# Evictions a step later, two sigmoid buffers, and conv coefficients on GpSimd in a hybrid encoder block

## The reference, cut to what matters

```
z = rms_norm(h)                     # h: 16 meta tokens + 4096 positions, 1024 channels, batch 4
v, gate, u = split(z @ w_in)        # 512 channels each
# conv group
c = v * sigmoid(gate)
c = depthwise_conv(c, width 31)     # along the sequence
conv_out = silu(layer_norm(c))
# S5 group: 32 groups x 16 channels, 64 complex states each, two directions
state_l = lam_bar * state_(l-1) + b_bar u_l        # forward, and backward in the other direction
y = gelu(sum over directions of Re(c state) + d * u)
s5_out = y * sigmoid(y @ glu_w + glu_b)
h = h + concat(conv_out, s5_out) @ w_out
h = h + relu(rms_norm(h) @ w_ff1)^2 @ w_ff2
out = rms_norm(h), meta positions dropped
```

## Time and profile before

| | us |
|---|---|
| median of 3 runs (lowest, highest) | 953.47 (952.92, 954.14) |
| profiled execution | 954.79 |
| its span, slowest core (4); the others | 953.7; from 945.5 |
| TensorE busy in the span | 786.1 |
| VectorE, ScalarE, GpSimd busy | 504.8, 367.8, 389.9 |

### The profile page before, as it was taken

One profiled execution on the slowest core, in us unless ns is written; L12 is line 12 of the kernel. 1 busy time (PEld: TensorE's weight loads), 2 busy tenths in 40 slices (PEclk: granted clock), 3 DMA queues, 4 the chain that ended last, 5 costly groups with the idle time before them and its releaser, 6 DMA issues.

```text
span 953.7 us, 15698 instructions; the slowest of 8 cores (945.5 to 953.7 us)
## 1 busy us (share of the span) xinstructions
PE 786.1 (82%) x4515; PEld 391.0 (41%) x4584; DVE 504.8 (53%) x971; ACT 367.8 (39%) x596; POOL 389.9 (41%) x446
## 2 busy tenths in 40 slices
PE   1555556689795689579999999999999999999992
PEld 0332234346233357324554444444444444444440
DVE  5665771844887955344663344334334433443577
ACT  5977766544013344645662111211121121112353
POOL 4767692781879342400005333423333243333230
PEclk9977778799996899779999999999999999999997
DMA  8477962654154937669605050501305050230134
GB/s 244 162 169 195 185 156 69 127 80 57 26 76 66 106 26 139 176 176 268 172 0 90 1 88 2 84 6 21 68 1 89 1 89 1 31 58 1 45 128 181
DMA packets 71955, 87.27 MB, mean 92 GB/s; under 512 B 7584, under 2 KB 55840, under 8 KB 71872
## 3 DMA queue, kind: packets, MB, share of 16 engines
q1 hardware_dynamic: 56752, 66.18, 29.9%
q0 software_dynamic: 14400, 19.76, 13.2%
q10 hardware_dynamic: 720, 0.33, 0.1%
HBM read 86.56 MB, written 19.45 MB: 111 GB/s over the span
## 4 chain that ended last, share of the span: by engine, by line
PE 65%; DVE 12%; issue 9%; ACT 5%; DMA 4%; SPq 3%; POOL 2%; DVEq 0%; ACTq 0%; POOLq 0%
PE p_pb L1134 23%; PE p_pb L1154 22%; PE p_pb L1080 6%; DVE p_pb L470 3%; PE p_pb L442 3%; PE p_pb L1003 3%; SPq L162 3%; DVE s_vo L470 2%; DMA s_xt<-xl 2%; PE p_pb L833 2%; PE p_pb L683 1%; DVE s_cd L470 1%; PE p_pb L922 1%; DVE s_vf L470 1%; ACT s_zt L349 1%
## 5 line engine op out<-in xcount | busy, mean ns | idle before, releaser
L470 DVE TENSOR_TENSOR s_h<-s_h,p_pb 128x512 f32<-128x512 f32 x288 | 197.4, 686 | 261.0 <-PE p_pb L1154 246.0
L470 POOL TENSOR_TENSOR s_hid<-s_rl 128x512 bf16<-128x512 f32 x128 | 133.6, 1047 | 322.6 <-ACT s_rl L1142 318.3
L1154 PE MATMUL p_pb<-s_w2c,s_hid 128*128 128x512 bf16 x1005 | 225.7, 379 | 5.5 <-DVE s_h L470 4.5
L1134 PE MATMUL p_pb<-s_zf,s_w1c 128*128 128x512 bf16 x1002 | 224.9, 379 | 1.2
L1142 ACT ACTIVATE s_rl<-p_pb 128x512 f32<-128x512 f32 x128 | 76.0, 597 | 327.8 <-PE p_pb L1134 320.2
L1154 PEld LDWEIGHTS p_pb<-s_w2c,s_hid 128*128 128x128 bf16 x1024 | 99.5, 98 | 126.7 <-issue 8.3
L1134 PEld LDWEIGHTS p_pb<-s_zf,s_w1c 128*128 128x128 bf16 x1024 | 100.1, 98 | 120.1
L442 PE MATMUL p_pb<-s_zsl,s_winu 128*128 128x512 bf16 x243 | 74.2, 456 | 2.3 <-ACT s_stsp L449 1.0
L372 PE MATMUL p_pb<-s_ident,s_zt 128*128 128x128 bf16 (+1 forms) x264 | 24.9, 250 | 55.5 <-ACT s_zt L358 42.4
L833 PE MATMUL p_pb<-s_zsl,s_winv 128*128 128x512 bf16 x250 | 58.3, 386 | 9.8 <-DVE s_usc L847 7.4
L372 PEld LDWEIGHTS p_pb<-s_ident,s_zt 128*128 128x128 bf16 (+1 forms) x264 | 20.0, 114 | 68.2 <-issue 67.2
(11 more groups left out here) (169 smaller groups left out, 951.5 us busy)
## 6 DMA issues: line engine op xcount, KB each, us to landing
s_xt<-xl SPq DMA_DIRECT2D x32, 512.0 KB, 5.9
s_h<-xl SPq DMA_DIRECT2D x16, 512.0 KB, 17.5
s_w1c<-w_ff POOLq DMA_DIRECT2D x8, 1024.0 KB, 11.7
s_w2c<-w_ff POOLq DMA_DIRECT2D x8, 1024.0 KB, 11.3
out<-s_h SPq DMA_DIRECT2D x15, 512.0 KB, 2.6
s_wstv<-w_in SPq DMA_DIRECT2D x4, 1024.0 KB, 10.2
s_kf<-scr_rs SPq DMA_DIRECT2D x8, 384.0 KB, 18.0
s_wstu<-w_in SPq DMA_DIRECT2D x4, 512.0 KB, 11.7
```

The costliest lines, as they stand in the source:

```text
L470: op(eng, lambda e: e.tensor_tensor(o, a, b_, op=o_), r=r, w=w)
L1134: op("pe", lambda e, k=k, f=f: e.matmul(pb[pi_][:, :], w1c[fc % 2][:, k, f * 128:(f + 1) * 128], zf[:, k, b * 512:(b + 1) * 512], start=(k ...
L1154: op("pe", lambda e, f=f, half=half: e.matmul(pb[pi_][:, :], hid[hb][:, f, ti * 128:(ti + 1) * 128], w2c[fc % 2][:, f, half * 512:(half + ...
```

## The change

- **Evictions.** The copies of `ust` and `wb` on ScalarE are put in a list `evq` and emitted one step later, behind norm_z and norm_sq of that step. `u_chunk` stands directly behind those and ahead of the due `wb_rows`. The DRAM write and read of a chunk follow its eviction, so they come a step later too. Far `v_pair` moves from steps 22 to 25 to steps 23 to 26.
- **Tail.** Three vg_chunks stand ahead of `v_pair` own and not four; the special columns stand behind it. The other 13 follow with `vpump(7)`.
- **Sigmoid.** Two buffers in turn; the second lies over `cmat`, which GpSimd's `cw` products read.
- **Strips.** The two directions overlap in 16 columns; they are now summed in PSUM, so a strip takes one copy of 496 columns and one small addition on VectorE where there were two.
- **Conv coefficients.** Three buffers, the third over a table of the tile loop. The groups are made a pair earlier; q = 2 and 3 on VectorE, q = 4 to 7 on GpSimd (before: 5 and 7 on GpSimd). Groups 0 and 1 are mixed into the first 24 carry operations only.

The diff, cut to its core:

```diff
@@ -430,6 +430,12 @@
     ucnt = [0]
+    evq = []
+
+    def evicts(kind=None):
+        for e in [e for e in evq if kind is None or e[0] == kind]:
+            evq.remove(e)
+            e[1]()
 
@@ -451,13 +457,14 @@
         us, uk = ust[c], "ust%d" % c
-        if ev == "act":
+
+        def evict():
             op("act", lambda e: e.copy(us[:], pb[bi][:]), r=[pbk[bi]], w=[uk])
-        else:
-            op("dve", lambda e: e.tensor_copy(us[:], pb[bi][:]), r=[pbk[bi]], w=[uk])
-        after(1, lambda: bounce_write(name, us[:], uk, b, c))
-        if c == 3:
-            after(2, lambda: bounce_read(name, uf if kind == "far" else uo[:, :, 2:258], name, b))
+            after(1, lambda: bounce_write(name, us[:], uk, b, c))
+            if c == 3:
+                after(2, lambda: bounce_read(name, uf if kind == "far" else uo[:, :, 2:258], name, b))
+
+        evq.append(("u", evict))
 
@@ -620,6 +627,7 @@
     def wb_rows(d, m, q, ws, wk):
+        evicts("w")
         bi = 6
@@ -629,7 +637,7 @@
         dst = wb[d][:, m, :, 4 * q:4 * q + 4, :].rearrange("p r a x -> p a r x")
-        op("act", lambda e: e.copy(dst, src), r=[pbk[bi]], w=["wb%d_%d_%d" % (d, m, q)])
+        evq.append(("w", lambda: op("act", lambda e: e.copy(dst, src), r=[pbk[bi]], w=["wb%d_%d_%d" % (d, m, q)])))
 
@@ -823,7 +831,8 @@
     usc = [sb("usc%d" % i, [128, 512], BF16, SG + 2048 + 1024 * i) for i in range(2)]
-    sgt = sb("sgt", [128, 512], F32, SG)
+    sgts = [sb("sgt%d" % i, [128, 512], F32, (SG, CMO)[i]) for i in range(2)]
+    vgn = [0]
 
@@ -835,16 +844,18 @@
         gb, vb = banks
-        op("act", lambda e: e.activation(sgt[:, 0:n], pb[gb][:, 0:n], AF.Sigmoid), r=[pbk[gb]], w=["sgt"])
+        sgt, sk = sgts[vgn[0] % 2], "sgt%d" % (vgn[0] % 2)
+        vgn[0] += 1
+        op("act", lambda e: e.activation(sgt[:, 0:n], pb[gb][:, 0:n], AF.Sigmoid), r=[pbk[gb]], w=[sk])
         if between is not None:
...
             dst = stsp[:, :, c, :].rearrange("p s k -> p k s")
-            op("dve", lambda e: e.tensor_tensor(dst, src, sg_, op=ALU.mult), r=[pbk[vb], "sgt"], w=["stsp"])
+            op("dve", lambda e: e.tensor_tensor(dst, src, sg_, op=ALU.mult), r=[pbk[vb], sk], w=["stsp"])
             return
-        op("dve", lambda e: e.tensor_tensor(usc[c % 2][:], pb[vb][:], sgt[:], op=ALU.mult), r=[pbk[vb], "sgt"], w=["usc%d" % (c % 2)])
+        op("dve", lambda e: e.tensor_tensor(usc[c % 2][:], pb[vb][:], sgt[:], op=ALU.mult), r=[pbk[vb], sk], w=["usc%d" % (c % 2)])
         after(1, lambda: bounce_write("uc", usc[c % 2][:], "usc%d" % (c % 2), b, c))
@@ -863,7 +874,7 @@
             e0 = 1 if d == 1 else 0
-            o0 = 0 if d == 1 else 256
+            o0 = 0 if d == 1 else 240
             for ri in range(2):
@@ -879,12 +890,9 @@
     def strip_copy(i, bi):
-        src = bass.AP(pb[bi], 0, [[512, 128], [272, 2], [1, 240]])
         dst = rs[:, i, :]
-        dst2 = bass.AP(rs, i * 496, [[8 * 496, 128], [256, 2], [1, 240]])
-        op("act", lambda e: e.copy(dst2, src), r=[pbk[bi]], w=["rs%d" % i])
-        tt("dve", dmsk[:, i, :], pb[bi][:, 240:256], dmsk[:, i, :], ALU.add, [pbk[bi], "dmsk", "rs%d" % i], ["dmsk"])
-        tt("dve", dst[:, 240:256], pb[bi][:, 256:272], dmsk[:, i, :], ALU.add, [pbk[bi], "dmsk"], ["rs%d" % i])
+        op("act", lambda e: e.copy(dst, pb[bi][:, 0:496]), r=[pbk[bi]], w=["rs%d" % i])
+        tt("dve", dst[:, 240:256], pb[bi][:, 240:256], dmsk[:, i, :], ALU.add, [pbk[bi], "dmsk"], ["rs%d" % i])
 
@@ -899,10 +907,10 @@
     cwx = sb("cwx", [128, 32, 40], BF16, WB2 + 10240)
-    cdb = [sb("cd%d" % i, [128, 4, 40, 16], BF16, WB2 + 5120 * i) for i in range(2)]
+    cdb = [sb("cd%d" % i, [128, 4, 40, 16], BF16, WB2 + 5120 * i if i < 2 else BBO) for i in range(3)]
 
     def cd_gen(q, eng="dve"):
-        i = q % 2
+        i = q % 3
         for dg in range(4):
@@ -920,9 +928,9 @@
                 op("pe", lambda e, g=g, d=d, dg=dg: e.matmul(
-                    pb[bi][:, 256 * dg:256 * dg + 256], cdb[q % 2][:, g % 4, 8 * d:8 * d + 8, :], uc[:, g, d:d + 256],
+                    pb[bi][:, 256 * dg:256 * dg + 256], cdb[q % 3][:, g % 4, 8 * d:8 * d + 8, :], uc[:, g, d:d + 256],
                     start=(d == 0), stop=(d == 4)),
-                   r=["cd%d" % (q % 2)] + uck, w=[pbk[bi]], sig=(dg == 1 and d == 4))
+                   r=["cd%d" % (q % 3)] + uck, w=[pbk[bi]], sig=(dg == 1 and d == 4))
         for dg in range(2):
@@ -1289,12 +1297,13 @@
             norm_sq(n + 2)
-
-        while late:
-            late.pop(0)[0]()
+        evicts()
         if uq:
...
             u_chunk(kd, ub, c, "act")
+
+        while late:
+            late.pop(0)[0]()
         if n in (2, 3):
@@ -1329,7 +1338,8 @@
                 do_wb(0)
-            if 22 <= n < 26:
+            if 23 <= n < 27:
+                evicts("w")
                 for _ in range(2):
@@ -1338,15 +1348,16 @@
                         push(f, 650)
-            if n >= 26:
+            if n >= 27:
                 cw_pump(2 if n % 2 else 1, 1)
-            if n >= 26 and len(bg) < 4 and wb_list:
+            if n >= 27 and len(bg) < 4 and wb_list:
                 do_wb(1)
...
     while uq:
+        evicts()
         u_chunk(*uq.pop(0), "act")
@@ -1354,24 +1365,23 @@
     nv = 0
-    while bg or late or wb_list or cw_list or cq or nv < 4:
+    while bg or late or wb_list or cw_list or cq or nv < 3:
+        evicts()
         while late:
...
             do_wb(1)
-        if vq and nv < 4:
+        if vq and nv < 3:
             vg_chunk(*vq.pop(0), (1, 5), lambda: pump(3500))
...
         tick()
+    evicts()
     tick()
...
     special_put(uo, "uo")
-    for c in range(4):
-        vg_chunk("sp", 0, c, (1, 5) if c % 2 else (0, 4))
-    special_bounce("c")
 
@@ -1395,7 +1405,8 @@
     sa, sb_, sab = Scan("dve", 0, 16, tmp, "cxa"), Scan("dve", 16, 20, tmp, "cxa"), Scan("dve", 0, 20, tmp, "cxa")
-    dq = zipped([ops_of(sab.carry), ops_of(lambda: [cd_gen(0), cd_gen(1)])])
+    dq = ops_of(sab.carry)
+    dq = zipped([dq[:24], ops_of(lambda: [cd_gen(0), cd_gen(1)])]) + dq[24:]
     dq = ops_of(sa.local) + ops_of(sb_.local) + dq
@@ -1404,12 +1415,13 @@
 
+    for c in range(4):
+        vg_chunk("sp", 0, c, (0, 1) if c % 2 else (2, 3))
+    special_bounce("c")
     nb = 0
     while vq:
-        if nb == 0:
-            uc_read(0)
         kb = vq[0]
-        vg_chunk(*vq.pop(0), ((0, 1), (2, 3))[nb % 2], lambda: vpump(10))
+        vg_chunk(*vq.pop(0), ((0, 1), (2, 3))[nb % 2], lambda: vpump(7))
         nb += 1
@@ -1426,8 +1438,8 @@
     for i in range(16):
-        if i % 2 == 0 and i >= 2 and i // 2 + 1 < 8:
-            cd_gen(i // 2 + 1, ("dve", "pool")[i // 2 in (4, 6)])
+        if i % 2 == 0 and i // 2 + 2 < 8:
+            cd_gen(i // 2 + 2, "dve" if i < 4 else "pool")
         conv_pair(i, i % 2)
```

## The result

The changed kernel is faster: 925.14 us median against 953.19, ratio 0.9703 with a 95% interval of 0.9683 to 0.9722, that is 28.3 us (26.5 to 30.2) less. The forecast was 922.5 us, in a range of 911 to 938. (One of the four executions of the changed kernel, 951.96 us, had a disturbed die and is left out of the ratio.) The profiled execution took 924.33 us with a span of 923.3 on core 0, where the sum against the profiled execution before had said 923.8.

A forecast was written before the change was run, and what follows sets the result against it. TensorE was taken to bound 65% of the span, with movable time before 428 us. Loop -10, tail -6 and conv with scan -15 gave -31 on 954.79, 923.8, less 1.3: 922.5 us, range 911 to 938.

The forecast's parts named there:

- Tile loop: Tile loop, 20 to 196 us: some 19 us of savings, part taken back through GpSimd; 10 us gain taken, bounds 2 to 19.
- x load: Tile loop: the x load now starts ahead of the far states' bounce read in SP's order, 2 us gained.
- read of uf: Tile loop: the DMA wait of the far states, 5.55 us, shrinks by about 2.5 us as v_pair moves a step later.
- Tail: Behind the tile loop: v_pair own starts 6 us earlier, bounds 4 and 7, with the reads of uo deciding.
- second sigmoid buffer: Tail: its first use waits for GpSimd's last product; costed at nothing, at most 2.49 us.
- Scan stage and start of the conv: Scan starts 2.3 us later, last product at 289 instead of 292.48, conv at 299.4 instead of 302.89: 3.5 us earlier.
- Conv: Conv stage: only pair 6 waits for coefficients; ssm_out 15 us earlier with the later scan start included, bounds 4 to 16.5.
- price of a group: Conv: a GpSimd coefficient group takes 5.47 us even beside VectorE's corrections, ready 0.5 to 1 us before use; far bound 8.7.
- Rival 1: The tile loop gives only 2 us, as GpSimd, ScalarE and norm_z waits remain; 930.5 us, chance 0.20.
- rival 2 and 4: Conv at 8.7 us a group or late, 934 us (0.12); GpSimd's groups bound the conv, slower, 959 us (0.05).
- rival 5: Whole kernel: the change moves instructions and no time, waits only change names; 953 us, chance 0.04.
- Rival 3: Everything comes: 19 us in the loop, 7 in the tail, 16.5 in the conv; 911 us, chance 0.13.

The follow-up runs named there:

- e1: Kernel before plus only the tile-loop part of the change (late evictions, u_chunk's place, later far v_pair): ratio 0.9895, 10.0 us faster than before.
- e2: Kernel before with one edit, the u_chunk ahead of the due batches of rows, evictions in the same step: ratio 0.9908, 8.8 us faster than before.
- e5: Changed kernel with the due batches of rows ahead of the u_chunk again, evictions still a step later: ratio 0.9846, 13.6 us slower than the changed kernel.
- e11: Changed kernel with both evictions issued in their own step, u_chunk still ahead of the rows: ratio 0.9634, 6.6 us faster than the changed kernel.
- e4: Changed kernel with the old tail, four vg chunks and the special columns ahead of v_pair own: ratio 0.9757, 5.1 us slower than the changed kernel.
- e8: Changed kernel with the old strips (two halves, two additions) and one sigmoid buffer: ratio 0.9731, 2.7 us slower than the changed kernel.
- e3: Changed kernel with the old coefficient groups: two buffers, old schedule, only q = 5 and 7 on GpSimd: ratio 0.9840, 13.1 us slower than the changed kernel.
- e7: Changed kernel with all coefficient groups on VectorE, three buffers and new schedule kept: ratio 0.9839, 13.0 us slower than the changed kernel.
- e9: Changed kernel with every tile's copy out of PSUM on ScalarE from step 27 on: ratio 0.9704, 0.1 us from the changed kernel.
- e10: Changed kernel with six scan operations per chunk, pair 6's group ahead of the corrections, three groups on GpSimd: ratio 0.9694, 0.9 us faster than the changed kernel.
- e12: e11 with six scan operations per chunk and pair 6's group ahead of the corrections, four groups on GpSimd: ratio 0.9646, 5.4 us faster than the changed kernel.

## Why the prediction was right, step by step

- **Tile loop, 10 us: right in size, by e1 (10.0) and the slowest cores' last tile (10.9), and partly by luck.** That the place of the u_chunk matters is shown by e2 (8.8 alone) and e5 (13.6 lost), and its shadow of 3.9 us at a double step by the rows of e2. Three things were wrong. Half of the slowest core's gain is the x load, costed at 2 us; the cores that had not waited for x gained 4.5 and 5.3 us only. The later eviction was costed at nothing; it costs 6.6 us in all (e11), seen as 9.2 us of waits of the u_chunks for their bank and 5.8 us more for s_wb. And what I had named as the taker of the gain, a longer wait of TensorE on norm_z behind GpSimd's products, did not come: that wait fell, though ScalarE's own wait for GpSimd's norm operations grew from 12.6 to 16.7 us. That 19 less 9 came to the measured 10 is several errors that cancel.
- **The x load, 2 us, and the read of uf, 2.5:** both waits went nearly whole, 6.1 us (0.2 left) and 5.6 (none left). The x load's went with the u_chunk's place (e2: 0.8 us left), which the prediction had given to the later v_pair; the uf wait went with the later v_pair (e2: 4.9 left, e11: none).
- **Tail, 6 us:** v_pair own 5.3 us nearer to the first chunk, 5.1 by e4; it waits for uo as said. The second sigmoid buffer at nothing: e8 bounds it and the strips together at 2.7.
- **Scan stage and start of the conv:** 3.8 us against 3.5, and the last product within 0.1 us of the sum. Two terms behind it were off and cancel in part: the scan starts 0.8 us later behind v_pair own (11.9 us against 11.1) and not 2.3 (the prediction's own 3.2 less 1.4 would give 1.8), and VectorE waits 2.1 and 1.0 us for the writes of uc, which no term held.
- **Conv, 15 us with the scan stage:** 15.1 on the slowest cores, 17.0 by the medians; e3 gives 13.1 for the groups alone. The price of a group, 5.47, held at 5.44 with VectorE busy. The groups were ready 2.5 to 3.1 us before their use and not 0.5 to 1, so GpSimd did not pace the conv: behind pair 6 TensorE ran at its own pace. e7 shows that the move to GpSimd is needed; whether the third buffer is was not tested.
- **Rival 1** (the loop gives only 2) fell by e1; **rival 2 and 4** by the 5.44; **rival 5** by the result. Rival 3 named 19 us in the loop: e11 comes to 14.9 at the slowest cores' last tile (181.29 against 196.19) and to 10.4 by the medians.
- The parts add up to 10.0 + 5.1 + 13.1 = 28.2, and with e8's 2.7 to 30.9, against the measured 28.3. With half widths of 1.2 to 2.2 us in each of them that is no contradiction, and no proof that the parts add exactly.
- The changed kernel's median lies 2.6 us over the forecast (925.14 against 922.5). Of that 0.5 us is in the profile (924.33 against 923.8). The rest is which execution was profiled: that of before was taken as 1.3 us over its median, and that of the changed kernel is 0.8 us under its own.

Open: why six of the cores wait 1.8 to 6.1 us for the x load before and none waits more than 0.5 us after. The last tile of the slowest core stands at nearly the same time in the changed kernel (185.30), in e1 (185.33) and in e2 (185.13), which had looked like a common bound. Over all cores it is no such thing: 184.8 to 186.2, 183.3 to 186.2 and 180.7 to 185.2 us. What e9 shows is that VectorE's queue holds it in the changed kernel, and in e11 that queue starts the far reduction 3.7 us earlier (156.52 against 160.19 us) and the last tile comes 4.0 us earlier.

## What to carry to other kernels

When a wait holds up work that does not need it, move the work ahead of the waiting instruction; that alone gave 8.8 of the loop's 10.0 us, about half of it on the slowest core through a load that was no longer waited for. Moving the release of a buffer later is not its twin: it was part of the same edit and took 6.6 us away, hidden by the gain. Undo each half of such an edit alone, inside the finished kernel: e1 and e2 differ by 1.2 us, which is no difference, for the later eviction with the later v_pair; e11 says 6.6 us lost by the eviction, and only that run separates the two. Compare a landmark on all cores before you give its shift to a cause: the last tile's 10.9 us on the slowest cores was 6.6 by the medians. And when a stage gets shorter without the time moving (e9, e10), look for the transfer or the engine's total that stands behind it.

## What was not expected of the hardware

- GpSimd's 128x640 product takes 1.36 to 1.38 us (21.77 us for 16, 44.25 for 32), whether VectorE is idle or busy with products that take one input from PSUM, while its 128x192 product at 0.66 us would have made it 2.2: both with bf16 output, the smaller with f32 inputs. The price per element of one form did not carry to the other.
- With the output weights' load issued 6.3 us later (331.53 against 325.21), TensorE waited 7.4 us longer for the reads of s_mixs (e10). All eight cores of e10 show a longer way to the GLU (28.9 to 36.9 us from ssm_out), and six of eight in the changed kernel and in e12 the 26.2 us. That the load and the reads shared the DMA queues is a likely reason and is not shown: no run moved the load alone.
